# Compressed keys and values formed together in front of the first attention scores, gate products behind the second pair

## The reference, cut to what matters

```python
kc = jnp.einsum('bnlgd,lde->bnge', k_cmp[:, gidx] + cmp_pe[:, None, :], cmp_wk)
vc = jnp.einsum('bnlgd,lde->bnge', v_cmp[:, gidx] + cmp_pe[:, None, :], cmp_wv)
gates = jax.nn.sigmoid(ga.astype(jnp.float32))...
```

## Time and profile before

| what | value |
|---|---|
| median of three runs | 1276.33 us (1276.31 to 1277.69) |
| the profiled execution | 1275.76 us |
| its span in the trace | 1274.0 us |
| PE, DVE, ACT busy | 1168.5, 933.2, 589.5 us |
| mean granted clock of PE | 0.959 |
| bytes read from memory | 277.91 MB, 219 GB/s over the span |

### The profile page before, as it was taken

One profiled execution on the slowest core, in us unless ns is written; L12 is line 12 of the kernel. 1 busy time (PEld: TensorE's weight loads), 2 busy tenths in 40 slices (PEclk: granted clock), 3 DMA queues, 4 the chain that ended last, 5 costly groups with the idle time before them and its releaser, 6 DMA issues.

```text
span 1274.0 us, 19995 instructions
## 1 busy us (share of the span) xinstructions
PE 1168.5 (92%) x8366; PEld 1057.0 (83%) x8366; DVE 933.2 (73%) x1630; ACT 589.5 (46%) x968; POOL 74.4 (6%) x106
## 2 busy tenths in 40 slices
PE   2798789999998987999999989999989998999997
PEld 1687468899897975789999979999979977999996
DVE  5967848888786955589987688887765957765445
ACT  1534645344345445553544464454443365444443
POOL 0000000000000000069100000000000000000000
PEclk8899889999999998999999999999999998999999
DMA  9982324788893860257789637779742452665830
GB/s 375 360 355 81 162 106 156 307 308 320 279 336 129 347 240 9 102 213 281 292 212 388 248 130 279 292 290 279 277 155 96 109 160 101 240 234 203 200 133 33
DMA packets 40810, 280.83 MB, mean 220 GB/s; under 512 B 4736, under 2 KB 5264, under 8 KB 7952
## 3 DMA queue, kind: packets, MB, share of 16 engines
q1 hardware_dynamic: 37296, 269.27, 58.4%
q0 software_dynamic: 2416, 7.92, 2.1%
q10 hardware_dynamic: 1008, 2.37, 0.5%
HBM read 277.91 MB, written 1.10 MB: 219 GB/s over the span
## 4 chain that ended last, share of the span: by engine, by line
PE 69%; DVE 19%; ACT 5%; DMA 5%; issue 1%; SPq 0%; DVEq 0%; ACTq 0%
PE PS L408 69%; DVE LO L1351 5%; DMA raw<-WS 4%; DVE raw L1341 4%; ACT HI L940 2%; DMA SC<-scratch 1%; DVE TMP L1416 1%; DVE HLo L1411 1%; DVE TMP L1451 1%; DVE SC L1555 1%; ACT SC L940 1%; ACT HH L940 1%; ACT SQ L940 1%; DVE SC L1540 1%; DVE RS L1555 1%
## 5 line engine op out<-in xcount | busy, mean ns | idle before, releaser
L408 PE MATMUL PS<-HH,HI 128*128 128x256 f32 x1748 | 502.3, 287 | 26.1 <-ACT HH L940 22.3
L408 PE MATMUL PS<-HLo,HI 128*128 128x256 f32 x1748 | 503.1, 288 | 0.7 <-DVE HLo L1411 0.2
L408 PE MATMUL PS<-HH,LO 128*128 128x256 f32 x1748 | 499.5, 286 | 0.0
L1351 DVE TENSOR_TENSOR LO<-raw,HI 128x1024 fp32r<-128x1024 f32 x340 | 403.9, 1226 | 122.6 <-ACT HI L940 122.4
L940 ACT ACTIVATE HI<-raw 128x1024 fp32r<-128x1024 f32 x340 | 339.9, 1048 | 90.8 <-PE PS L408 60.2
L408 PEld LDWEIGHTS PS<-HH,HI 128*128 128x128 f32 x1748 | 340.5, 195 | 35.2 <-DVE LO L1351 19.3
L408 PEld LDWEIGHTS PS<-HH,LO 128*128 128x128 f32 x1748 | 340.2, 195 | 3.3 <-issue 0.5
L408 PEld LDWEIGHTS PS<-HLo,HI 128*128 128x128 f32 x1748 | 339.7, 194 | 3.7 <-DVE HLo L1411 2.7
L1341 DVE CUSTOM_DVE_ANT_0 raw<-raw,CB,SM 128x1024 f32<-128x1024 f32 x168 | 210.5, 1285 | 22.3 <-DMA raw<-WS 22.2
L408 PE MATMUL PS<-HI,HDH 128*128 128x512 f32 x352 | 140.2, 398 | 0.0
L408 PE MATMUL PS<-HI,HDL 128*128 128x512 f32 x352 | 139.5, 396 | 0.0
(11 more groups left out here) (230 smaller groups left out, 1038.0 us busy)
## 6 DMA issues: line engine op xcount, KB each, us to landing
raw<-WS SPq DMA_DIRECT2D x255, 1024.0 KB, 5.9
SC<-scratch POOLq DMA_DIRECT2D x2, 1024.0 KB, 13.3
FB<-gates_out POOLq DMA_DIRECT2D x3, 512.0 KB, 4.7
SQ<-gates_out POOLq DMA_DIRECT2D x3, 512.0 KB, 9.6
X<-xT ACTq DMA_DIRECT2D x1, 1024.0 KB, 6.8
SC<-ssm POOLq DMA_DIRECT2D x2, 512.0 KB, 4.4
out<-TMP SPq DMA_DIRECT2D x2, 512.0 KB, 2.6
CB<-vecs SPq DMA_DIRECT2D x1, 512.0 KB, 6.4
```

What stands on the lines that cost most here:

```text
L408: return e.matmul(o, l, r, start=start, stop=stop, skip_group_check=True)
L1351: e.tensor_tensor(LO[:, s % HL, :], raw_half(j, h), HI[:, s % HL, :].bitcast(fp32), O.subtract).then_inc(*D.up(("lo", s)))
```

## The change

The plan puts the raw chunk behind ab5: ab5, cmp, mod 12, ab6, mod 13, ab7, mod 14, mod 15 and so on. Before, it stood behind mod 14.

```diff
-    plan += weave(ws("ab", 8), am[:7], 0) + [("raw", ("cmp", 0))] + am[7:] + ws("abo", 4)
+    ab = weave(ws("ab", 8), am[:7], 0)
+    ab.insert(ab.index(("w", ("ab", 5))) + 1, ("raw", ("cmp", 0)))
+    plan += ab + am[7:] + ws("abo", 4)
```

On PE one block of 32 matmuls forms keys (to PSUM partitions 0 to 63) and values (64 to 127) in turn, ahead of the loop and behind ab7. The gate products move into pass 1. A short block in pass 0 spreads the second group's keys and transposes the values:

```diff
+            def cmp_inputs():
+                walk.weight(("cmp", 0), 0)
+                ps = take("ck")
+                w.wait_ge(*loaded(cmp_j))
                 w.wait_ge(*D.at(("zc", 1)))
                 for j in range(16):
-                    i = mm(ps[0:15, g * 64:g * 64 + 64], ZC[:, 1, j, g, :], cmp_w[:, 1, j, :], g == 0 and j == 0,
-                           j == 15)
+                    for t in range(2):
+                        i = mm(ps[64 * t:64 * t + 64, 0:30], cmp_w[:, t, j, :], ZC[:, t, j, :, :], j == 0, j == 15)
+                i.then_inc(*P.up("ck", "cmp_used"))
+                walk.done(("cmp", 0), 0)
+                banks.give("ck")
+            def cmp_spread():
+                ps = take("cv")
+                w.wait_ge(*A.at("kt1"))
+                mm(ps[64:128, 144:159], C("ident")[0:64, 0:64], kt1, True, True)
+                for g in range(2):
+                    i = e.transpose(ps[0:15, g * 64:g * 64 + 64], vt1[:, g * 15:g * 15 + 15], C("ident")[64:128, 64:128])
+                i.then_inc(*P.up("cv"))
-            compressed = {1: [cmp_keys], 2: [lambda: cmp_values(0), lambda: cmp_values(1)],
-                          3: [lambda: cmp_scores(0)], 4: [lambda: cmp_scores(1)],
+            compressed = {0: [cmp_spread], 1: [gate_values], 3: [lambda: cmp_scores(0)], 4: [lambda: cmp_scores(1)],
...
+            cmp_inputs()
             for p in range(9):
                 scores("ab", AB, p)
```

ACT copies the three results of the first block, 64 rows by 15, 15 and 30, ahead of its loop. It copies those of the spread behind the exponentials of block 0, and makes the gates' exponential behind those of block 1. On DVE the windows are written behind ab3 and ab4, the walk's account of the raw chunk is closed ahead of the loop, and the two gate instructions come between `biased` and `scaled` of pass 1:

```diff
-            for n in (6, 7):
+            for n in range(8):
                 use(("ab", n), 0)
                 use(("ab", n), 1)
-                cmp_windows(n - 6)
+                if n in (3, 4):
+                    cmp_windows(n - 3)
+            low(walk.weight(("cmp", 0), 0))
+            walk.done(("cmp", 0), 0)
             gate("f0", 16, 1.0, S("nw")[:, 8:16])
...
-            compressed = {1: [cmp_chunk], 2: [lambda: walk.done(("cmp", 0), 0)],
-                          3: [lambda: cmp_bias(0)], 4: [lambda: cmp_scale(0), lambda: cmp_bias(1)],
+            compressed = {3: [lambda: cmp_bias(0)], 4: [lambda: cmp_scale(0), lambda: cmp_bias(1)],
                           5: [lambda: cmp_scale(1)]}
             for p in range(9):
                 for i in (2 * p, 2 * p + 1):
                     biased("ab", i, *AB[i])
+                if p == 1:
+                    gate_values()
```

More of the change, by code:

```diff
@@ L322, in build @@
         ge = sqf[0:24, 1400:1656]
-        kt1 = sqf[0:64, 1656:1671]
+        kt1, vt1 = sqf[0:64, 1656:1671], sqf[64:128, 1656:1686]
         wgh, wgl = [x[:, 0, 0:192].rearrange("p (k n) -> p k n", k=8) for x in (HDH, HDL)]
@@ L668, in pe, with gate_values @@
             values_only(("ab", 7))
[L669 to L683, removed]
             cmp_j = where["cmp", 0]
             cmp_w = rawt[:, cmp_j % RAW, :].rearrange("p (s j e) -> p s j e", s=2, j=16)
-            def cmp_keys():
+            def gate_values():
+                ps = take("gates")
+                w.wait_ge(*D.at("gatew"))
+                for k in range(8):
+                    mm(ps[0:24, 0:256], wgh[:, k, :], HH[:, k, :], k == 0, False)
+                    mm(ps[0:24, 0:256], wgl[:, k, :], HH[:, k, :], False, False)
+                    i = mm(ps[0:24, 0:256], wgh[:, k, :], HLo[:, k, :], False, k == 7)
+                i.then_inc(*P.up("gates"))
+                banks.give("gates")
+                ps = take("gates2")
+                w.wait_ge(*A.at(("free", "gates")))
+                w.wait_ge(*CONST.at("in"))
+                for qt in range(2):
+                    i = e.transpose(ps[:, qt * 24:qt * 24 + 24], ge[:, qt * 128:qt * 128 + 128], C("ident")[0:24, 0:24])
+                i.then_inc(*P.up("gates2"))
+                banks.give("gates2")
+            def cmp_inputs():
                 walk.weight(("cmp", 0), 0)
@@ L691, in cmp_keys @@
                 w.wait_ge(*loaded(cmp_j))
[L692 to L699, removed]
                 w.wait_ge(*D.at(("zc", 1)))
                 for j in range(16):
-                    i = mm(ps[0:15, g * 64:g * 64 + 64], ZC[:, 1, j, g, :], cmp_w[:, 1, j, :], g == 0 and j == 0,
-                           j == 15)
[L704 to L709, removed]
+                    for t in range(2):
[10 more added lines that the diff above has]
+                i.then_inc(*P.up("cv"))
+                banks.give("cv")
             def cmp_scores(qt):
@@ L1126, in act, with gate_values, cmp_inputs, cmp_spread @@
             values_only(("ab", 7), 128, ("fm", "ab"))
-            w.wait_ge(*P.at("gates"))
-            fn(ge, bank("gates")[0:24, 0:256], F.Exp, scale=-1.0).then_inc(*A.up(("free", "gates")))
-            def cmp_keys():
+            def gate_values():
+                w.wait_ge(*P.at("gates"))
+                fn(ge, bank("gates")[0:24, 0:256], F.Exp, scale=-1.0).then_inc(*A.up(("free", "gates")))
+            def cmp_inputs():
                 high(walk.weight(("cmp", 0), 0))
+                walk.done(("cmp", 0), 0)
                 w.wait_ge(*P.at("ck"))
[L1133 to L1137, removed]
+                fn(kt1, bank("ck")[0:64, 15:30], F.Copy).then_inc(*A.up())
+                fn(KC[0:64, :], bank("ck")[0:64, 0:15], F.Copy).then_inc(*A.up())
+                fn(vt1, bank("ck")[64:128, 0:30], F.Copy).then_inc(*A.up(("free", "ck"), "kt1"))
+            def cmp_spread():
                 w.wait_ge(*P.at("cv"))
-                fn(KC[64:128, :], bank("cv")[64:128, 128:143], F.Copy).then_inc(*A.up("kc"))
+                fn(KC[64:128, :], bank("cv")[64:128, 144:159], F.Copy).then_inc(*A.up("kc"))
                 fn(VC[0:15, :], bank("cv")[0:15, 0:128], F.Copy).then_inc(*A.up(("free", "cv"), "vc"))
@@ L1152, in cmp_turn @@
                     .then_inc(*A.up(("free", ("ct", qt, hh))))
-            compressed = {1: [cmp_keys], 2: [cmp_values], 3: [lambda: cmp_exp(0)], 4: [lambda: cmp_exp(1)],
+            compressed = {3: [lambda: cmp_exp(0)], 4: [lambda: cmp_exp(1)],
                           5: [lambda: cmp_turn(0, 0), lambda: cmp_turn(0, 1)],
                           6: [lambda: cmp_turn(1, 0), lambda: cmp_turn(1, 1)]}
+            cmp_inputs()
             for p in range(9):
@@ L1163, in act @@
                     exps("ab", i, *AB[i])
+                    if i == 0:
+                        cmp_spread()
+                    if i == 1:
+                        gate_values()
                 high(walk.spare(2))
@@ L1572, in dve @@
                 .then_inc(*D.up("gatew"))
-            for n in range(6):
-                use(("ab", n), 0)
-                use(("ab", n), 1)
             pe2 = S("pe").unsqueeze(2).unsqueeze(3).to_broadcast([128, 16, 2, 15])
@@ L1584, in cmp_windows, with gate_values @@
                     e.tensor_tensor(ZC[rows, s], win, pe2[rows], O.add).then_inc(*D.up(("zc", s)))
-            for n in (6, 7):
+            for n in range(8):
                 use(("ab", n), 0)
                 use(("ab", n), 1)
-                cmp_windows(n - 6)
[L1590 to L1594, removed]
-            gate("f0", 16, 1.0, S("nw")[:, 8:16])
+                if n in (3, 4):
+                    cmp_windows(n - 3)
+            low(walk.weight(("cmp", 0), 0))
+            walk.done(("cmp", 0), 0)
+            gate("f0", 16, 1.0, S("nw")[:, 8:16])
+            def gate_values():
+                w.wait_ge(*P.at("gates2"))
+                e.tensor_scalar(GT, bank("gates2")[:, 0:48], 1.0, None, O.add).then_inc(*D.up(("free", "gates2")))
+                w.wait_ge(*D.now())
+                e.reciprocal(GT, GT).then_inc(*D.up())
+                w.wait_ge(*D.now())
             def cmp_bias(qt):
@@ L1625, in cmp_scale @@
                 e.tensor_tensor(s3, s3, gg.unsqueeze(2).to_broadcast([128, 8, nk]), O.mult).then_inc(*D.up(("cp", qt)))
-            def cmp_chunk():
-                low(walk.weight(("cmp", 0), 0))
-            compressed = {1: [cmp_chunk], 2: [lambda: walk.done(("cmp", 0), 0)],
-                          3: [lambda: cmp_bias(0)], 4: [lambda: cmp_scale(0), lambda: cmp_bias(1)],
+            compressed = {3: [lambda: cmp_bias(0)], 4: [lambda: cmp_scale(0), lambda: cmp_bias(1)],
                           5: [lambda: cmp_scale(1)]}
```

## The result

The changed kernel took 1281.73 us (median of 7 runs, 1280.23 to 1285.39) against 1276.33 us before (median of 7, 1273.82 to 1277.69). The medians lie 5.4 us apart. The forecast was 1285.3 us, with a range from 1281.5 to 1289.0, and the time lies 0.2 us inside its lower end. The sign and the mechanism of the loss hold. The size was too large. The profiled execution took 1280.90 us, its span 1279.1 (before 1274.0).

The account below looks back on a forecast made before the run. DVE was taken to bound the attention passes, with free time only ahead of them. Pass 6 would start 9.0 us later; carried to the end, 1276.33 + 9.0 = 1285.3 us, range 1281.5 to 1289.0.

Parts of the forecast that it names:

- The sign and the mechanism of the loss: Whole kernel: slower, chance 0.92, because mod loads wait behind the raw chunk and their products move into the attention.
- The order of the stream: Passes 0 to 5: mods 14 to 19 wait for PE's release; twelve DVE products where there were two, +12.1 us.
- 39.8 us: From mod 14's landing to pass 6: DVE's remaining work 24.6 us, plus gates 0.7 and twelve products 14.5.
- The new block: PE ahead of the first scores: 32 matmuls, keys and values alternating between column halves, 64 records in 2.1 us.
- The bound of 4.1 us: New block's upper bound, 64 records at 64 ns, column halves not at once; as a rival 1287.3 us, chance 0.08.
- The wait for mod 14: Pass 0: mod 14 issued at 104.6, landing 6.15 us later at 110.75; DVE stands 2.3 us from 108.4.
- the windows' 4.09 us: Ahead of the attention: DVE's window instructions move into its wait for ab6 and ab7, cost nothing; at most 4.09 us.
- 150.5: Start of pass 6: landing 110.75 plus 39.8 gives 150.55, 9.0 us later than 141.55 before.
- The sum of the prediction: Up to pass 6: +12.1 +2.3 +0.7 -3.7 -1.5 -0.8 = +9.1; by the landing, 9.0 us later.
- I carry 9.0 us to the end: From pass 6 on: both kernels do the same in the same order, so the 9.0 us stay to the end.
- a gain by the clock: Rival behind the attention: PE's low-clock stretch falls elsewhere, some 2.8 us come back, 1282.5 us; chance 0.08.
- The gates in pass 1: Pass 1: PE's 2.7 us lie behind scores 1 and beside DVE's work; two DVE instructions add 0.7 us.

Follow-up runs that it names:

- Run 3: The kernel before with only the plan's new order, and three mod halves per pass in place of two: 1284.61 us, ratio 1.0076.
- run 1: The changed kernel with the plan's old order, the raw chunk again behind mod 14: 1276.65 us, ratio 1.0022.
- run 5: The changed kernel with the new block's 16 keys matmuls first, then the 16 for values, not in turn: 1284.13 us, ratio 1.0074.
- Run 6: As run 1, with DVE's instruction that releases the f0 gate row's transfer moved from ahead of the loop into pass 2: 1271.77 us, ratio 0.9973.
- 7: As Run 6, with mod products only from pass 1 on and PE filled by 28 products of zeros ending pass 2: 1276.17 us, ratio 1.0004.
- runs 8 and 9: PE filled with products of zeros in its last two attention pauses: 8 the kernel before, 1272.57 us, ratio 0.9981; 9 the changed kernel, 1283.25 us, ratio 1.0052.
- runs 2: As run 1, with mod products allowed only from pass 1 on: 1272.11 us, ratio 0.9983.
- Run 4: The changed kernel with mod products allowed only from pass 1 on: 1280.08 us, ratio 1.0042.

## Why the prediction was right, and where its size was off

**The order of the stream: right.** SP, the order of DVE's products, twelve of them in passes 0 to 5, and the empty time before are as written. Run 3 has the loss with the plan's order alone, and in run 1 undoing the order alone takes 3.4 us off the time and 5.8 us off pass 6. From the landing of mod 14 to pass 6 the forecast had 39.8 us, and the trace has 39.6 (111.19 to 150.82).

**The new block: right.** 2.1 us forecast, 2.06 measured, and run 5 gives the price without the pairing: 3.71 us for the block and a landing 1.4 us later. The bound of 4.1 us was a little high.

**The wait for mod 14: mis-sized.** The step took 6.15 us for the transfer, from the one that followed the same wait before. It was 4.80, and DVE stood 1.09 us in place of 2.3. In the kernel before POOL had begun to read the gate row at 118.2, 2.4 us ahead of that burst (its row of POOL is `118.20 0.56 POOL L1937`). Run 6 shows that POOL's transfers delay such a burst; that they made these 1.35 us I infer and did not test.

**The front: not in the sum.** PE's second flips, from which on the change can act, began at 77.48 and at 79.19 us in the two profiled executions:

```profile
77.48 5.40 PE L408 MATMUL PS<-SC 128*128 128x512 f32 x8 [2.55 <-DMA SC<-scratch]
```

```profile
79.19 5.40 PE L410 MATMUL PS<-SC 128*128 128x512 f32 x8 [2.73 <-DMA SC<-scratch]
```

Those 1.7 us are no effect of the change: the filled kernel before has them too (79.56), and runs 1 to 6 don't. They go with PE's clock in the projections, which from 45.70 to 49.10 was 1.00 in the one and 0.50 in the other. All four executions with late flips (changed, 7, 8, 9) have the lower clock there, and the other nine have 1.00:

```profile
45.70:49.10 3.40, 3.40 (x31) 3.40 (x30) 3.40 (x5) 2.30 (x3) 0.00 (x0) 1.00 0.77 275
```

```profile
45.70:49.10 3.40, 3.40 (x18) 3.40 (x17) 3.40 (x5) 1.74 (x2) 0.00 (x0) 0.50 0.80 267
```

From the flips to the last record of ab7 both take 24.9 us, so the windows' 4.09 us cost nothing, as forecast. The agreement of 150.82 with 150.5 is in part luck. Of the 9.3 us by which pass 6 is late, 1.7 come from the front, and 7.6 lie between the flips and pass 6, 71.6 against 64.1 us, where the change is. The sum of the prediction with the measured transfer gives it: 9.0 less 1.35 is 7.65. That it fits so closely is luck too, since the filled pair of runs 8 and 9, with the same work up to there, has 10.1 us (73.7 against 63.6).

**"I carry 9.0 us to the end": the step that failed.** The lag of the profiled execution is 9.3 us at the first output parts, 6.7 at the first new rows (189.67 and 196.34), 5.1 at the third layer's and at the end. The forecast named this as a rival with 0.08 (a gain by the clock, 1282.5 us), and that is what came. The output product of the changed kernel ran at the full clock, where the earlier trace rows has 0.50:

```profile
173.80:183.60 9.80, 9.14 (x48) 6.18 (x48) 4.10 (x4) 4.57 (x7) 0.00 (x0) 1.00 0.19 59
```

Runs 8 and 9 show that this is the cause of the first drop. With the clock held up in both, the lag of the changed kernel is 10.5 us at pass 6 (143.13 and 153.60) and still 10.4 at the first new rows:

```profile
188.64 1.28 DVE L1462 SCALAR_TENSOR_TENSOR X<-TMP,NR,X 128x1024 f32<-128x1024 f32 x1
```

```profile
199.07 1.28 DVE L1473 SCALAR_TENSOR_TENSOR X<-TMP,NR,X 128x1024 f32<-128x1024 f32 x1
```

Another 1.7 us go between 402 and 530 us, where both kernels do the same. PE was at the lower clock three times there in the kernel before (from 467 to 471, 477 to 488 and 512 to 515 us), and twice in the changed one (479 to 489 and 517 to 520). The one more found PE busy nearly all the time:

```profile
467.30:470.70 3.40, 3.28 (x24) 2.97 (x24) 1.17 (x8) 0.00 (x0) 0.00 (x0) 0.50 0.00 0
```

3.4 us at half the clock are 1.7 us of work at the full one. No run holds the clock up there, so that this is the cause is read from two traces and not tested. This part of the program also differs between other executions: it took 127.6 us before, 125.9 in the changed kernel and 131.4 in runs 2 and 8, which had 27 us of the lower clock in it. So the 5.1 us of the profiled pair are 1.7 in the front and 7.6 up to pass 6, less 2.6 at the end of the attention and 1.7 between 402 and 530 us, to the rounding. How the clock falls in the passes themselves also differs between executions: PE was at the lower clock for 17 us in one piece, from 120.5 on, in the filled changed kernel, which needed 73.7 us to pass 6, and for 10 us, from 117.5 on, in the unfilled one, which needed 71.6.

**The gates in pass 1: partly hidden.** Their two DVE instructions cost 0.7 us as forecast. Run 4 adds that their PE part is covered only by mod 14's wait and products; without these DVE waits 1.6 us for it.

## What to carry to other kernels

A buffer ring that one queue fills in a fixed order is held by its slowest user. Moving one chunk forward moves every later load behind that user's release, and here it took ten products of 1.2 us from DVE's free time into the stage that DVE bounds. Before such a move, write down for each later chunk which wait now stands ahead of its load, and what the engine that consumes it does at that time.

## What the runs showed of the hardware

- POOL waited 9.6 to 9.9 us for a write of 4 KB to memory, asked for as 1024 elements of 4 bytes, in the rows above. While it ran in run 1, five loads of 1 MiB asked for by another queue moved almost nothing until 111 us, and the first landed 9.8 us after its issue; with the write elsewhere it was 4.9 us.
- PE's two column halves take records of 64 weight and 30 moving columns in turn at 32 ns each (run 5's pair: 2.06 us for 64), and at 58 ns each when one half gets all of its own first (3.71 us).
- Filling PE with products of zeros in real pauses raised the granted clock of the product behind them from 0.68 to 1.00 and took its 34 records from 9.00 to 6.40 us. Another filling, in pass 2, ran partly at the lower clock, took 4.90 us in place of 3, and held up the scores behind it.
- Where PE's clock fell differed between executions of kernels with the same work at that place. The part from 402 to 530 us took from 125.9 us (13.7 us of it at the lower clock) to 131.4 us (27.3 us), a difference as large as the whole effect of the change.
